# The last layer's final residual of a two-layer decoder step: one of three token groups made on GpSimd

## What is computed

```python
def rmsnorm(x, g):
    xf = x.astype(jnp.float32)
    y = xf * lax.rsqrt(jnp.mean(xf * xf, axis=-1, keepdims=True) + EPS)
    return (y * g.astype(jnp.float32)).astype(x.dtype)
...
    x = x + rmsnorm(mix, nm_post)
    hf = jnp.einsum('btd,df->btf', rmsnorm(x, nf_pre), w_up)
    f = jnp.einsum('btf,fd->btd', jnp.square(jax.nn.relu(hf)), w_down)
    x = x + rmsnorm(f, nf_post)
```

## Time and profile before

| | us |
|---|---|
| median of 3 runs (2672.02 to 2673.41) | 2673.11 |
| the profiled execution | 2667.48 |
| its span, first to last instruction | 2665.7 |
| busy in it: TensorE | 2597.1 |
| VectorE | 1106.1 |
| GpSimd | 759.4 |
| ScalarE | 686.0 |

### The profile page before, as it was taken

One profiled execution on the slowest core, in us unless ns is written; L12 is line 12 of the kernel. 1 busy time (PEld: TensorE's weight loads), 2 busy tenths in 40 slices (PEclk: granted clock), 3 DMA queues, 4 the chain that ended last, 5 costly groups with the idle time before them and its releaser, 6 DMA issues.

```text
span 2665.7 us, 42179 instructions
## 1 busy us (share of the span) xinstructions
PE 2597.1 (97%) x17128; PEld 2357.8 (88%) x17128; DVE 1106.1 (41%) x1521; ACT 686.0 (26%) x1153; POOL 759.4 (28%) x359
## 2 busy tenths in 40 slices
PE   9999999999999999999999999999999999999996
PEld 7995666989999999999889866669899999999996
DVE  5456666264222222222665566652722222222226
ACT  3125555141100110010341355542501100100113
POOL 2431000303433443443123300003034434433440
PEclk9999999999999999999999999999999999999998
DMA  6114322321111111111331243222211111111113
GB/s 222 46 39 127 83 80 72 113 89 48 41 47 47 47 39 47 47 41 46 113 113 43 63 121 81 81 65 108 89 48 48 40 47 47 44 43 47 47 40 138
DMA packets 91492, 185.97 MB, mean 70 GB/s; under 512 B 29664, under 2 KB 42144, under 8 KB 91360
## 3 DMA queue, kind: packets, MB, share of 16 engines
q1 hardware_dynamic: 88656, 175.75, 20.5%
q0 software_dynamic: 2560, 8.39, 1.2%
q10 hardware_dynamic: 144, 0.00, 0.0%
HBM read 157.77 MB, written 23.11 MB: 68 GB/s over the span
## 4 chain that ended last, share of the span: by engine, by line
PE 91%; DVE 3%; ACT 3%; issue 1%; SPq 1%; DVEq 1%; DMA 0%; ACTq 0%
PE psum L1681 57%; PE psum L2154 7%; PE psum L1711 4%; PE psum L1871 3%; PE psum L1666 3%; PE psum L1897 3%; PE psum L1883 2%; PE psum L1774 2%; PE psum L1918 2%; PE psum L1730 1%; PE psum L1634 1%; ACT z L866 1%; PE psum L1931 1%; PE psum L1741 1%; PE psum L1950 1%; PE psum L1929 1%
## 5 line engine op out<-in xcount | busy, mean ns | idle before, releaser
L605 POOL TENSOR_TENSOR wh<-raw,ones 128x1024 fp32r<-128x1024 f32 x148 | 284.3, 1921 | 1265.6 <-PE psum L1681 1100.7
L1681 PE MATMUL psum<-hh,wh 128*128 128x352 f32 x2064 | 448.5, 325 | 0.2 <-issue 0.2
L1681 PE MATMUL psum<-hh,wl 128*128 128x352 f32 x2064 | 445.0, 323 | 0.0
L1681 PE MATMUL psum<-hl,wh 128*128 128x352 f32 x2064 | 444.5, 323 | 0.0
L607 POOL TENSOR_TENSOR wl<-raw,wh 128x1024 fp32r<-128x1024 f32 x148 | 407.0, 2750 | 21.4
L1022 ACT ACTIVATE z<-z 128x1056 f32<-128x1056 f32 x64 | 69.7, 1089 | 1208.1 <-DVE stat L1537 1199.5
L1681 PEld LDWEIGHTS psum<-hh,wl 128*128 128x128 f32 x2064 | 354.4, 188 | 0.0
L1681 PEld LDWEIGHTS psum<-hh,wh 128*128 128x128 f32 x2064 | 351.8, 189 | 2.7 <-issue 1.0
L1681 PEld LDWEIGHTS psum<-hl,wh 128*128 128x128 f32 x2064 | 350.4, 188 | 0.0
L1533 DVE SCALAR_TENSOR_TENSOR z<-psum,rinv 128x1056 f32<-128x1056 f32 x64 | 80.5, 1257 | 544.1 <-PE psum L1681 542.3
L1559 DVE TENSOR_TENSOR z<-psum,z 128x1056 f32<-128x1056 f32 x104 | 130.7, 1257 | 392.2 <-PE psum L1681 339.4
(11 more groups left out here) (242 smaller groups left out, 3519.3 us busy)
## 6 DMA issues: line engine op xcount, KB each, us to landing
raw<-wst SPq DMA_DIRECT2D x160, 512.0 KB, 3.3
z<-cache_c SPq DMA_DIRECT2D x352, 64.0 KB, 1.8
x<-x_spill SPq DMA_DIRECT2D x4, 4224.0 KB, 14.3
raw<-cache_c SPq DMA_DIRECT2D x160, 64.0 KB, 1.8
x_spill<-x SPq DMA_DIRECT2D x2, 4224.0 KB, 13.7
x_spill<-x SPq DMA_DIRECT2D x6, 1408.0 KB, 5.2
x<-xT SPq DMA_DIRECT2D x8, 528.0 KB, 8.3
yT<-x SPq DMA_DIRECT2D x6, 704.0 KB, 3.3
```

Source lines behind the costliest of these rows:

```text
L605: pool.tensor_tensor(wh[:, s, :], raw[:, s, :], ones[:, 0:1].to_broadcast([P, TW]), ALU.mult)
L1681: ins = pe.matmul(bank3(u, g), w[:, s, o:o + P], m[:, k, cols(g)], start=(k == 0 and n == 0), stop=(k == kk - 1 and n == 2))
```

## The change

In the last layer GpSimd makes the new residual of the middle group (group 1), in the same two halves of two operations each, behind its last weight tile. It waits for the loaded `x2` and for the ninth `root_full` of the layer, which is `rinv` of group 1, and counts each half in a new semaphore `x_last`. VectorE no longer makes group 1 there; in its place stands only the wait for that `root_full`, and then group 2. SyncE sends in the order (0,0), (0,1), (1,0), (2,0), (1,1), (2,1), where the two of group 1 wait for `x_last`. The first layer is as before.

```diff
@@ -264,6 +264,7 @@
         x_new = count("x_new", 2 * NX, NX)
+        x_last = sem("x_last")
@@ -573,9 +574,11 @@
-            for g in range(NG):
-                for h in range(2):
-                    sp.wait_ge(x_new.sem, Pos(DEPTH - 1).whole(x_new, NX + KD * g + KD // 2 * (h + 1)))
+            for g, h in ((0, 0), (0, 1), (1, 0), (2, 0), (1, 1), (2, 1)):
+                    if g == 1:
+                        sp.wait_ge(x_last, h + 1)
+                    else:
+                        sp.wait_ge(x_new.sem, Pos(DEPTH - 1).whole(x_new, NX + KD * (g // 2) + KD // 2 * (h + 1)))
                     own = slice(KD // 2 * h, KD // 2 * (h + 1))
                     sp.dma_start(yT.rearrange("k p t -> p k t")[:, own, cols(g)], x[:, own, cols(g)]).then_inc(s_out, 16)
@@ -674,6 +677,16 @@
+            last = Pos(DEPTH - 1)
+            pool.wait_ge(x_loaded.sem, last.whole(x_loaded, x_loaded.per))
+            pool.wait_ge(root_full.sem, last.whole(root_full, 9))
+            for h in range(2):
+                part = slice(KD // 2 * h, KD // 2 * (h + 1))
+                four = z[:, part, cols(1)]
+                pool.tensor_tensor(four, four, by_group(rinv, 1, KD // 2), ALU.mult)
+                pool.drain()
+                pool.tensor_tensor(x[:, part, cols(1)], four, x2[:, part, cols(1)], ALU.add).then_inc(x_last, 1)
@@ -1601,9 +1614,10 @@
                 after_f(2, 2)
-                if l == DEPTH - 1:
-                    new_x(1, 0, x2)
-                new_x(1, 1, x2)
+                if l < DEPTH - 1:
+                    new_x(1, 1, x2)
+                else:
+                    root()
                 for h in range(2):
                     new_x(2, h, x2)
```

## The result

| | before | after |
|---|---|---|
| median of 9 runs | 2670.65 (2667.82 to 2673.41) | 2679.44 (2677.21 to 2680.6) |
| ratio, 95% interval | | 1.0031 (1.0021 to 1.0041) |
| profiled execution's span | 2665.7 | 2675.8 |

The change makes the kernel slower, by 5.6 to 11 us on this comparison. A second one on another occasion, 11 runs against 33, gave 1.0022 (1.0013 to 1.0031). It is the last sum and the final residual, free of what TensorE did earlier. Before it ran from 2645.47 to 2661.98 + 3.3, 19.8 us; after, from 2649.98 to 2671.49 + 3.9, 25.4 us.

A forecast was written before the change was run, and what follows sets the result against it. VectorE bounds the tail: moving four operations gains 4.2 us at best, but three GpSimd operations among four adds delay the memset 8.8, giving +4.5 on 2673.11: 2677.6 us, range 2674.3 to 2680.5.

The forecast's parts named there:

- the alternation: At the last layer's end, GpSimd operations and VectorE's two-input SBUF adds take turns; +4.5 us, chance 0.80.
- rival (c): GpSimd starts late, so all four of its operations fall among group 2's adds; +7.5 us, 2680.6, chance 0.07.
- What bounds the tail: After TensorE's last product, VectorE's work bounds the end, from 2648.93 to 2661.95 us.
- GpSimd's price: Each 128x1408 operation moved to GpSimd takes 3.24 us, with bounds 2.60 and 3.55.
- near tie of GpSimd's second operation and the first add: GpSimd's add issues at 2646.40, VectorE's first `sacc` add at 2646.46; with VectorE first, +4.4 instead of +4.5 us.
- Rival (a): The engines do not hinder each other at the tail; the 4.2 us gain comes through, 2668.9, chance 0.07.
- the narrow reading of the two-port rule: GpSimd blocks only VectorE instructions in two-port mode, so fp32 two-tensor products would be free; time 2668.9.
- Rival (b): Group 2's four adds keep their turn, GpSimd getting in only once; +2.2 us, 2675.3, chance 0.06.
- `rinv` of group 2 keeps its 2.15 behind the memset: After VectorE's later signal, sum and `rinv` take as long as before: 2.15 us, ready at 2659.85.
- Cost nothing: In SyncE's output queue the new order adds no time; the last transfer still lands in 3.3 us.
- no issue moves behind a late one: GpSimd's halves, done by 2649.6 and 2656.6, are ready before group 2's two halves in the output queue.
- the case to which I gave 0.80, within 0.2%: The whole kernel's time changes by less than about 0.2% (5.3 us), indistinguishable from no change; chance 0.80.

The follow-up runs named there:

- m1: Kernel before, but GpSimd makes only the multiply of group 1, half 0, output in the old order; ratio 0.9995, tail 18.2 us.
- m2: As m1, with group 2's squares in PSUM for VectorE's adds; ratio 0.9994 against the kernel before, tail 18.2 us.
- l1: Changed kernel, with GpSimd waiting until VectorE has signalled group 2's sum; ratio 1.0021 against the kernel before, tail 25.5 us.
- p1: Changed kernel, with group 2's last-layer squares written to PSUM, so the four adds read one operand there; ratio 1.0004 against the kernel before, tail 21.8 us.
- w2: Changed kernel, with 19 unused products on TensorE between its last product and the last partition sum; one profiled run, tail 24.7 us.
- o1: Changed kernel, with SyncE sending the output in the old order; ratio 1.0016 against the kernel before, tail 24.8 us.
- g1: Kernel before, no GpSimd work added: VectorE makes group 1, half 0, ahead of the last take_down; ratio 0.9994, median 2669.60 us.
- h1: Changed kernel halved: GpSimd makes only group 1, half 0, output in the old order; ratio 0.9996 against the kernel before, tail 20.6 us.
- n1: Kernel before with one more semaphore that nobody uses; ratio 0.9999, tail 19.8 us.
- h2: As h1, with group 2's squares in PSUM; ratio 0.9989 against the kernel before, tail 18.6 us.

## Why the prediction was right, and where it was short

Predicted was +4.5 us, 2677.6, with a range of 2674.3 to 2680.5, and the likeliest case was the alternation. The median is 2679.44, inside the range, and the mechanism is the one that ran: the tail grew by 5.6 us.

That the number fell inside the range was in part luck. The range was built on a median before of 2673.11, from three runs; over nine runs it is 2670.65. On that base the forecast would have been 2675.2 and the upper end 2678.0, and 2679.44 would lie outside. It is also above 2679.1, where the forecast's own range ended; only the room that was left for rival (c), which did not happen, took it in. The first comparison moved by 8.8 us, nearly twice the 4.5, the second by 5.7. By its steps:

- **What bounds the tail** was read rightly: VectorE's list, in which `rinv` of group 2 stood ready unused. m1 and m2 show it from the other side: one operation less is 1.6 us less in the tail.
- **GpSimd's price.** Taken 3.24, bounds 2.60 and 3.55; measured 3.16 in the second operation, which waited for nothing, and 3.15 in l1's first. The first operation's 3.19 includes a wait: it was issued at 2647.60, and VectorE's add (2646.07, 1.63 long) held the port until 2647.70, as the sum had it. The Trainium skill's figure ("GPSIMD Engine Reference", performance versus the Vector engine), scaled to this length, was an estimate of 3.09; the measured 3.16 lies between it and my line. The 4.1 that the prediction gives for that figure leaves the first operation at its old length; with all four shortened the same walk gives 3.9.
- **The alternation** came as written, the near tie of GpSimd's second operation and the first add included (0.04 us apart, GpSimd first). Expected were adds of some 3 us and a memset 8.8 us later; measured 3.51, 3.31, 3.29 and 8.5 later, the difference being mostly GpSimd's operations of 3.16 instead of 3.24.
- **Rival (a)**, no hindrance, is out, since three adds of 0.53 took over 3 us each. With it goes the narrow reading of the two-port rule in the Trainium skill ("Advanced Engine Details and Errata", VectorE performance modes). p1 marks the line: with one operand in PSUM the adds are free. The Trainium skill has in "SBUF — State Buffer", two separate sides, that the pair of ports is locked for a whole instruction, two-input ones included. The trace agrees, with 3.3 us for a 0.53 add.
- **Rival (b)**, the adds keeping their turn, is out: three of four waited for an operation each. **Rival (c)**, a late start, is out: GpSimd began 0.14 after its `rinv`, following 32.90 us without work.
- **"`rinv` of group 2 keeps its 2.15 behind the memset"** failed: it was 2.82. I had moved the sum later without asking what TensorE does meanwhile. After 12.21 us without work the sum ran at a granted clock of 0.50 and took 1.54 for 0.86. w2 gives the 0.7 us back. The 2.15 was not safe even without the delay: in m1 the sum took 1.54 after the same 3.67 us as before.
- **The output queue, "Cost nothing"**, failed, and with it "no issue moves behind a late one". I checked that GpSimd's data would be ready in time, but not what stands ahead of its transfer. The order of the change puts (1,1) behind (2,0), which VectorE finishes only at 2668.23, so a transfer that could have left at 2660.9 left beside the last one. o1 shows 0.6 us.

The later memset (8.5), the later `rinv` (0.7), the four operations that left VectorE, as far as the prediction counted them (-4.2), and the slower landing (0.6) add up to 8.5 + 0.7 - 4.2 + 0.6 = 5.6, and 5.6 is what the tail shows, twice. That is 0.21%, just over the bound of 0.2%. So the case to which I gave 0.80, within 0.2%, did not come: both ratios (1.0031 and 1.0022) lie above it, though the interval of the second, from 1.0013 on, does not exclude it.

## What to carry to other kernels

Before moving an elementwise operation to GpSimd, count not what VectorE is rid of but how many of its remaining two-input SBUF operations stand in that time. Each of them, however short, can wait for a whole GpSimd operation, and the short ones on the path to a signal are the dearest. What was safe beside GpSimd here is work of VectorE with an operand in PSUM (p1, m2) or no work at all (m1); one operation put into such a stretch took 1.6 us off the tail, four added 5.6. And when a chain is delayed, look at what its later links do meanwhile: TensorE, after 12.21 us without work, came back at half its clock, and a queue in fixed order held what was ready behind what was not.

## What the runs showed of the hardware that I had not expected

A VectorE operation that waits for GpSimd ends after it by its own time less about 0.14: the first add ends 0.39 behind GpSimd's end (0.53 alone), the operations of 128x1408 in l1 some 1.48 behind (1.62 alone). The same partition sum took 1.54 after 6.05 us (g1), 7.67 us (h1) and 12.21 us without work, and 0.76 and 0.86 in the two runs in which TensorE had been given work to within 1.02 us of it. After 3.65 to 3.67 us it was anything from one to the other: 0.86 in the kernel before, n1 and l1, 1.03 in h2, 1.27 in p1, 1.35 in m2 and 1.54 in m1. So the same stop costs 0.7 us in one execution and nothing in another. And the stretch around 204 to 212 us is granted 1.00 in some executions and 0.57 to 0.79 in others, of kernels that are identical there. In the changed kernel's profile 2.6 us arose at that stretch and 1.6 us at 1320 to 1330 us, which is why the tails were compared here and not the spans.
